# Two blocks of the recurrent branch multiplied between the sparse heads: two transformer blocks in fp32 on one core

## The chip, the core and the metric

One core of a Trainium2 chip runs the whole program. The metric is the device time of one execution in microseconds. Of the kernel before, three runs are shown, with their median.

## What is computed

The reference runs two blocks over 256 tokens of width 1024. The first has a gated and an attention layer, each with a mixture of experts. The second, which matters here, has two layers of feed-forward, hybrid mixer, feed-forward. The mixer projects the normalised tokens once and feeds three branches:

```python
proj = h @ w_in
ret_p, dsa_p, rwkv_p, gate_p = split_cols(proj, GROUP_SIZES)
y_ret  = retention(...)
y_dsa  = sparse_attention(...)      # 8 heads of 64, each query keeps its 64 best keys
y_rwkv = rwkv7_time_mix(rwkv_p, mu, ...)   # recurrent branch
merged = g_ret * (y_ret @ p_ret) + g_dsa * (y_dsa @ p_dsa) + g_rwkv * (y_rwkv @ p_rwkv)
return merged @ w_out
```

`rwkv_p` is 1792 columns of the projection, and the recurrent branch first mixes each of its columns with that of the token before (`p + mu * (prev - p)`). This projection does not depend on the sparse attention.

## The kernel before

The five engines run hand-written streams in fixed order: `pe_...` is TensorE, `v_...` VectorE, `s_...` ScalarE, `g_...` GpSimd and `sp_...` the sync engine's queue. Nothing is scheduled at run time; an engine waits on a semaphore and everything behind it in its stream waits too.

**Weights.** A block is 1024 x 256 weights (1 MB), loaded by the sync queue into a ring of five slots, in a fixed order of jobs; the load of job n goes out when job n-5 has been multiplied, which GpSimd tells the queue (`freed`, L532). The products are made in fp32 out of three reduced products: ScalarE copies the block into a rounded "high part" (`s_part_high`, L2049, the copy at L2058; three buffers, so the high part of load n waits for the product of load n-3), VectorE subtracts it from the weights and leaves the "low part" in the slot (`v_part_low`, L2060, at L2066). `s_ahead(m)` and `v_ahead(m)` (L2078, L2083) do that for load m: "a split" is VectorE's part. TensorE waits for it in `pe_parts`.

**Pieces.** Four PSUM banks are used in turn. Each product that TensorE makes takes the next bank (`take`), after a wait until the piece that had it four pieces ago was read out (`s_free`). Every engine counts all the pieces, and `skip(n)` passes over those that another engine reads. Two more banks hold the sums of the sparse values.

**A block of the branch.** `pe_chan` (L2123) multiplies one block: 2 x 8 x 3 matmuls of 128x128 by 256 columns into one bank. VectorE reads it in `v_shifted_channels` (L3163; two instructions at L3171, two at L3176) with the mixing of neighbours. There are seven such blocks, loads 24 to 30. The first is multiplied between the first two score pairs of the sparse heads, the other six in `pe_rwkv`, after the heads.

**The sparse heads** (`pe_sparse`, L2670; `s_sparse`, `v_sparse`). For heads 0 to 7 in pairs p = 0 to 3:

- `score(p)` makes two pieces, the scores of two heads (`pe_score_pair`, L1168, matmuls of 64x128 by 256);
- VectorE's `softmax_head(h)` adds the mask (L2775, then the bank is free), takes the maximum (L2778) and negates it (L2780);
- ScalarE's `exponential(h)` (L2714) makes the probabilities;
- "the turning" of a head (`pe_turned`, L1182, the transposes at L427) makes one piece, which ScalarE copies out (L2726);
- `values(p)` multiplies the turned probabilities of a pair with the values, in the two banks of the sums.

TensorE's order is score 0, block, score 1, then for each p: turning of heads 2p and 2p+1, values p-1, score p+2; then values 3 and `pe_to_heads`, which spreads the reciprocals of the sums over the channels in two pieces ("the spreading"; it waits for VectorE's reciprocal, L2795). VectorE goes: softmax 0 and 1, read of the first block, softmax 2 to 7, split of load 26, reciprocal. ScalarE's high part 26 (job 26) is made before the exponentials, that of load 27 after the last copy.

Behind the heads the six blocks follow each other in `pe_rwkv` (L2868, the loop at L2887), and in `v_rwkv` (L3180) VectorE takes in turn the split of the load that is wanted two blocks on and the read of a block.

Of the kernel before, what the change touches and what calls it, by code (L numbers as in the profile page):

```python
# [52 lines left out]
DH = 8  # L53
# [23 lines left out]
RW_CHUNKS = 14  # L77
# [122 lines left out]
def build(nc, a, out, regions=("A", "moe0", "B", "moe1", "two"), layers_two=LAYERS):  # L200
    (c1_at, _), (c2_at, _) = constants()
    NC = max(max(v[1] for v in c1_at.values()), max(v[1] for v in c2_at.values()))
    with ExitStack() as ctx:
# [431 lines left out]
        def heads2(b):  # L635

            return ps[:, b, :].rearrange("p (t n) -> p t n", n=BLK)
# [1341 lines left out]
        XLM = lay(KC, SEQ, of=W_parts)  # L1979
# [98 lines left out]
        def s_ahead(*loads):  # L2078
            for m in loads:
                s_part_high()  # L2080
                s.other_jobs(whole_after.get(m, 0))

        def v_ahead(*loads):  # L2083
            for m in loads:
                v_part_low()
                v.other_jobs(whole_after.get(m, 0))
# [583 lines left out]
        def pe_sparse():  # L2670

            pe.e.wait_ge(s_v2p, pe.c["v2p"].next())
            pe.to_channels(DT, KC)
            for n in range(4):

                pe.e.wait_ge(s_free[(pe.pieces.n - 1 - n) % BANKS], pe.read_out(pe.pieces.n - 1 - n))
            pe_scores(range(IH), lambda h: DCT[rows_of(h), 5 + h // 2, :], lambda h: DCT[rows_of(h), 7, :])

            pe_merge_retention()

            def score(p):
                pe_score_pair(p, lambda h: DCT[rows_of(h), h // 2, :], dkey)

            def values(p, turned):
                return pe_value_pair(p, turned,
                                     lambda h: ps[rows_of(h), 4 + h // 4, (h // 2 % 2) * SEQ:(h // 2 % 2 + 1) * SEQ],
                                     lambda h, jt: DTV[:, jt, :], DPTR)

            score(0)
            pe_chan((XH, XLM))  # L2690
            score(1)
            pe.e.wait_ge(s_acc_free, pe.c["accf"].next())
            for p in range(DH // 2):
                turned = [pe_turned(DPRB[:, h]) for h in (2 * p, 2 * p + 1)]
                if p:
                    values(p - 1, held)
                held = turned
                if 2 * p + 4 < DH:
                    score(p + 2)
            values(DH // 2 - 1, held).then_inc(s_acc_full, 1)  # L2700
            pe_to_heads(RCP_TOK)

        def s_sparse():
            copy_channels(s, 0, DCT, KC)
            s.skip(IH)
            s_merge_retention()
            s_ahead(26)
            s.skip(5)

            def exponential(h):  # L2710

                s.e.wait_ge(s_v2a, s.c["v2a"].next())
                for t in range(T):
                    last = nc.scalar.activation(DPRB[:, h, t, :], DSB[:, h % 2, t, :], ACT.Exp, bias=NMX[:, h, t:t + 1],  # L2714
                                                accum_out=LSUM[:, h, t:t + 1])
                last.then_inc(s_exp, 1)

            exponential(0)
            exponential(1)
            for p in range(DH // 2):  # L2720
                for h in (2 * p, 2 * p + 1):
                    if h + 2 < DH:
                        exponential(h + 2)
                    b = s.take()
                    s.e.wait_ge(s_full[b], s.filled())
                    nc.scalar.activation(DPTR[:, h % 4], heads2(b), ACT.Copy).then_inc(s_free[b], 1)  # L2726
                if 2 * p + 4 < DH:
                    s.skip(2)
            s.skip(2)

        def v_sparse():
            BUF["scores"], BUF["ptr"] = DSB, DPTR
            copy_channels(v, 1, DCT, KC)
            for h in range(IH):
                b = v.take()
                v.e.wait_ge(s_full[b], v.filled())
                nc.vector.tensor_scalar(RL[:, :, :], heads2(b), HD ** -0.5, 0.0, ALU.mult, ALU.max).then_inc(s_free[b], 1)
                v.sync()
                for t in range(T):
                    if h == 0:  # L2740
                        nc.vector.tensor_scalar(IS[:, t, :], RL[:, t, :], WI[:, t, h:h + 1], None, ALU.mult)
                    else:
                        nc.vector.scalar_tensor_tensor(IS[:, t, :], RL[:, t, :], WI[:, t, h:h + 1], IS[:, t, :],
                                                       ALU.mult, ALU.add)
                v.sync()
            causal = tab(c2_at, "causal", SEQ)
            nc.vector.tensor_tensor(IS[:, :, :], IS[:, :, :], causal, ALU.add)
            v.sync()

            src = IS  # L2750
            for i in range(TOPK // 8):
                for t in range(T):
                    nc.vector.max(TOP8[:, t, :], src[:, t, :])
                v.sync()
                for t in range(T):
                    nc.vector.match_replace(WORKD[:, t, :], TOP8[:, t, :], src[:, t, :], PAD_LOW)
                v.sync()
                src = WORKD
                v_ahead(18 + i)
                if i % 2:  # L2760
                    v_merge_retention(i // 2)
            nc.vector.tensor_tensor(MASK[:, :, :], WORKD[:, :, :], IS[:, :, :], ALU.not_equal)
            v.sync()
            nc.vector.tensor_scalar(MASK[:, :, :], MASK[:, :, :], -NEG, NEG, ALU.mult, ALU.add)
            v.sync()
            nc.vector.tensor_tensor(MASK[:, :, :], MASK[:, :, :], causal, ALU.add)
            v.sync()
            def softmax_head(h):

                b = v.take()  # L2770
                v.e.wait_ge(s_full[b], v.filled())
                if h >= 2:

                    v.e.wait_ge(s_exp, v.c["exp"].next())
                nc.vector.scalar_tensor_tensor(DSB[:, h % 2], heads2(b), SCALE, MASK[:, :, :],  # L2775
                                               ALU.mult, ALU.add).then_inc(s_free[b], 1)
                v.sync()
                nc.vector.tensor_reduce(MX[:, h, :], DSB[:, h % 2], AX.X, ALU.max)  # L2778
                v.sync()
                nc.vector.tensor_scalar(NMX[:, h, :], MX[:, h, :], -1.0, None, ALU.mult).then_inc(s_v2a, 1)  # L2780

            softmax_head(0)
            softmax_head(1)
            v_shifted_channels(0)
            softmax_head(2)
            softmax_head(3)
            for p in range(2, DH // 2):
                v.skip(2)
                softmax_head(2 * p)
                softmax_head(2 * p + 1)  # L2790
            v_ahead(26)
            v.skip(4)

            v.e.wait_ge(s_exp, v.c["exp"].next(2))
            nc.vector.reciprocal(RCP_TOK.rearrange("p t h -> p h t"), LSUM[:, 0:DH, :]).then_inc(s_v2p, 1)  # L2795
            v.e.wait_ge(s_acc_full, v.c["acc"].next())
            for i in range(2):
                b = v.take()
                v.e.wait_ge(s_full[b], v.filled())
                nc.vector.tensor_copy(flat(RATES[:, :, :]), ps[:, b, :]).then_inc(s_free[b], 1)  # L2800
                v.sync()
                last = nc.vector.tensor_tensor(flat(YTS[:, 2 * i:2 * i + 2, :]), ps[:, 4 + i, :], flat(RATES[:, :, :]),
                                               ALU.mult)
                v.sync()
            nc.vector.nop().then_inc(s_acc_free, 1)

        def g_sparse():
            g.skip(4 + IH)
            g_merge_retention()
            g.skip(2)  # L2810
            g.freed()
            g.skip(2 * DH - 2 + 2)
            g.c["acc"].n += 1


# [52 lines left out]
        def pe_rwkv():  # L2868
# [15 lines left out]
                        last.then_inc(s_gates, 1)  # L2884
                gates_done[0] += count

            for _ in range(RW_CHUNKS // 2 - 1):  # L2887
                pe_chan((XH, XLM))
            pe.e.wait_ge(s_acc_free, pe.c["accf"].peek())
            pe_merge_sparse(0)  # L2890
# [181 lines left out]
            pe.e.wait_ge(s_v2p, pe.c["v2p"].next())  # L3072

        def s_rwkv():
            s.skip(6)
            s_ahead(*range(27, 34))

            s.e.wait_ge(s_v2a, s.c["v2a"].next())
            nc.scalar.activation(LR[0:64, 0, :], LR[0:64, 0, :], ACT.Tanh)
# [98 lines left out]
            last.then_inc(s_free[b], 1)  # L3178

        def v_rwkv():  # L3180
            for c in range(2, RW_CHUNKS, 2):
                v_ahead(26 + c // 2)
                v_shifted_channels(c)
            v.sync()
# [183 lines left out]
            v_part_low()  # L3368

        def g_rwkv():  # L3370
            for _ in range(6):
                g.freed()
            g_merge_sparse(0)
            g.skip(1 + 6 + 4 + 2)
            g_merge_sparse(1)
            g.skip(2)
            g_merge_sparse(2)
            g_merge_sparse(3)
            n_levels = int(math.log2(CH))
            g.skip(6 + WH + 2 + 6 * (n_levels - 2) + 4 + 4 + 6 * N_CH - 4 + 5)  # L3380
# [220 lines left out]
```

## Time and profile before

| | |
|---|---|
| median of 3 runs | 2798.08 us (2797.85 to 2803.94) |
| profiled execution | 2798.51 us, its span 2796.7 us |
| TensorE busy (matmuls) | 2599.5 us, 93% |
| VectorE busy | 1274.0 us, 46% |
| ScalarE busy | 836.0 us, 30% |
| sparse heads and what follows, first layer | from 1576 us on |
| the same, second layer | from 2362 us on |

The profile is of one execution. Times in a timeline are microseconds from the span's start. A group of matmuls starts when its first starts; its last ends some 0.2 us after the next group could start, as matmuls are pipelined, so lengths are best taken from start to start. In square brackets stands how long the engine was idle before, and which engine's instruction ended that. The granted clock (PEclk) is in parts of full speed. A row of the view by stretches has the stretch, its length, the busy time (and number of instructions) of TensorE's matmuls, its weight loads, VectorE, ScalarE and GpSimd, then the clock, the share of the DMA engines' time and the GB/s. A row of DMA issues has the tile and its source, how many, the KB of each and the median time from issue to landing.

### The profile page before, as it was taken

To read this page: it belongs to the slowest core of one execution; us is meant where nothing else is said; L and a number is where in the kernel's file an instruction comes from. 1 tells how busy PE (TensorE), PEld (TensorE's weight loads), DVE (VectorE), ACT (ScalarE), POOL (GpSimd) and SP (SyncE) were. 2 spreads that over 40 slices of the span, in tenths; PEclk is the share of its full clock that TensorE was granted. 3 is DMA by queue.
4 is the path that set the end of the run, shared out by engine and by line. 5 is a ranking of instruction groups with operands and counts; after the bars stand their busy time and mean duration, and the time that the engine had idled before them with its cause. 6 is when DMAs were issued, how large, how long until landed. Compare 5 with 4: busy or idle time off the path is not lost.

```text
span 2796.7 us, 46123 instructions
## 1 busy us (share of the span) xinstructions
PE 2599.5 (93%) x19503; PEld 2008.1 (72%) x19503; DVE 1274.0 (46%) x1875; ACT 836.0 (30%) x1051; POOL 0.2 (0%) x4
## 2 busy tenths in 40 slices
PE   8899888879899888879999999999999999999998
PEld 8743433348543333369999899999899898899998
DVE  4610101037411000055566765655655658766555
ACT  4300000025210000033343442443433444523433
POOL 0000000000000000000000000000000000000000
PEclk9999999999999999999999999999999999999999
DMA  8689999973899999955563441455555544323553
GB/s 270 264 357 425 426 425 425 426 286 106 329 400 425 425 425 425 426 192 181 181 230 122 135 140 59 137 166 181 181 181 181 192 152 150 107 77 107 166 181 136
DMA packets 286519, 685.17 MB, mean 245 GB/s; under 512 B 11992, under 2 KB 217616, under 8 KB 236944
## 3 DMA queue, kind: packets, MB, share of 16 engines
q1 hardware_dynamic: 282792, 671.27, 63.6%
q10 hardware_dynamic: 3560, 11.45, 1.1%
q8 instruction: 132, 2.16, 0.3%
q14 instruction: 35, 0.29, 0.0%
HBM read 681.63 MB, written 1.05 MB: 244 GB/s over the span
## 4 chain that ended last, share of the span: by engine, by line
PE 69%; DMA 20%; DVE 6%; ACT 2%; issue 1%; DVEq 1%; SPq 0%; ACTq 0%; POOLq 0%
PE psum L419 68%; DMA weight_ring<-in_w_gate 14%; DMA weight_ring<-in_w_up 3%; DMA weight_ring<-in_w_down 2%; DVE weight_ring_parts L2066 1%; PE psum L427 1%; ACT weight_ring_parts L2058 1%; DVEq L552 1%; DMA weight_ring<-in_w_in_a 0%; DVE arena L3260 0%; SPq L1921 0%; DMA h_tok<-in_mem 0%; DMA weight_ring<-in_w_in 0%; DVE arena L1837 0%; DVE small L2778 0%
## 5 line engine op out<-in xcount | busy, mean ns | idle before, releaser
L419 PE MATMUL psum<-weight_ring_parts,arena_parts 128*128 128x256 f32 (+1 forms) x2992 | 666.4, 315 | 6.3 <-DVE arena_parts L2159 1.9
L2066 DVE TENSOR_TENSOR weight_ring_parts<-weight_ring,weight_ring_parts 128x2048 fp32r<-128x2048 f32 x217 | 496.5, 2290 | 338.0 <-ACT weight_ring_parts L2058 332.0
L419 PE MATMUL psum<-x_chan_parts,weight_ring_parts 128*128 128x256 f32 x3200 | 612.2, 282 | 12.9 <-DVE arena_parts L2155 7.7
L2058 ACT ACTIVATE weight_ring_parts<-weight_ring 128x2048 fp32r<-128x2048 f32 x217 | 414.9, 1913 | 465.7 <-POOLq L532 345.4
L419 PE MATMUL psum<-weight_ring,arena 128*64 128x512 f32 (+1 forms) x2112 | 474.8, 582 | 73.8 <-DMA weight_ring<-in_w_gate 39.1
L419 PEld LDWEIGHTS psum<-weight_ring_parts,arena_parts 128*128 128x128 f32 x2992 | 496.4, 189 | 42.9 <-issue 3.3
L419 PEld LDWEIGHTS psum<-x_chan_parts,weight_ring_parts 128*128 128x128 f32 x3200 | 509.0, 190 | 18.3 <-issue 12.9
L419 PE MATMUL psum<-arena 64*64 64x64 f32 (+7 forms) x4616 | 467.0, 335 | 29.3 <-DVE arena L1837 15.6
L419 PEld LDWEIGHTS psum<-weight_ring,arena 128*64 128x64 f32 (+1 forms) x2112 | 179.3, 140 | 361.4 <-issue 358.5
L419 PE MATMUL psum<-weight_ring_parts,x_chan_parts 128*128 128x256 f32 x2336 | 427.5, 285 | 2.3 <-DVE arena_parts L2155 2.2
L419 PE MATMUL psum<-arena_parts,weight_ring_parts 128*128 128x256 f32 x1536 | 419.0, 283 | 0.0
L419 PEld LDWEIGHTS psum<-arena 64*64 64x64 f32 (+3 forms) x4616 | 247.6, 141 | 227.9 <-issue 210.1
L419 PEld LDWEIGHTS psum<-weight_ring_parts,x_chan_parts 128*128 128x128 f32 x2336 | 359.3, 189 | 10.0 <-issue 7.8
L419 PEld LDWEIGHTS psum<-arena_parts,weight_ring_parts 128*128 128x128 f32 x1536 | 284.1, 189 | 1.3
L1853 DVE TENSOR_TENSOR arena<-arena,psum 128x512 f32<-128x512 f32 x32 | 22.0, 687 | 521.2 <-PE psum L419 519.9
L1837 DVE COPY arena<-psum 128x512 f32<-128x512 f32 x48 | 33.2, 691 | 296.9 <-PE psum L419 262.5
L1699 ACT ACTIVATE arena<-psum 128x512 f32<-128x512 f32 x32 | 19.1, 597 | 484.6 <-PE psum L419 484.6
L1692 ACT ACTIVATE arena<-psum 128x512 f32<-128x512 f32 (+1 forms) x80 | 34.3, 467 | 371.8 <-PE psum L419 335.0
L2066 DVE TENSOR_TENSOR weight_ring_parts<-weight_ring,h_tok_parts 128x2048 fp32r<-128x2048 f32 x32 | 73.3, 2291 | 66.6 <-ACT h_tok_parts L2058 65.8
L419 PE MATMUL psum<-arena_parts,h_tok_parts 128*128 128x256 f32 x320 | 90.2, 282 | 0.0
L419 PE MATMUL psum<-x_chan_parts,h_tok_parts 128*128 128x256 f32 x320 | 89.7, 280 | 0.0
L427 PE MATMUL psum<-tables,arena 128*128 128x128 f32 x472 | 69.9, 288 | 14.9 <-DVE arena_parts L2159 4.6
(324 smaller groups left out, 1713.6 us busy)
## 6 DMA issues: line engine op xcount, KB each, us to landing
weight_ring<-in_w_gate SPq DMA_DIRECT2D x92, 1024.0 KB, 23.2
weight_ring<-in_w_up SPq DMA_DIRECT2D x92, 1024.0 KB, 22.9
weight_ring<-in_w_in SPq DMA_DIRECT2D x70, 1024.0 KB, 5.0
arena<-in_w_down SPq DMA_DIRECT2D x64, 1024.0 KB, 22.5
weight_ring<-in_w_down SPq DMA_DIRECT2D x64, 1024.0 KB, 23.2
weight_ring<-in_ffa_w_in SPq DMA_DIRECT2D x44, 1024.0 KB, 7.1
weight_ring<-in_ffb_w_in SPq DMA_DIRECT2D x44, 1024.0 KB, 5.7
arena<-in_w_gate SPq DMA_DIRECT2D x36, 1024.0 KB, 18.5
```

Of the source, the lines that this page charges most:

```text
L419: return nc.tensor.matmul(*args, **kw)
L427: last = nc.tensor.transpose(ps[0:cols, b, lo:lo + rows], src, ident[0:rows, 0:rows])
L552: self.e.drain()
L1692: nc.scalar.activation(dst, ps[:, b, 0:dst.shape[1]], ACT.Copy).then_inc(s_free[b], 1)
L1699: nc.scalar.activation(SILU[:, half, :], ps[:, b, :], ACT.Silu).then_inc(s_free[b], 1)
L1837: nc.vector.tensor_copy(dst, ps[:, b, :]).then_inc(s_free[b], 1)
L1853: nc.vector.tensor_tensor(HG[:, half * 512:(half + 1) * 512], SILU[:, half, :], ps[:, b, :], ALU.mult).then_inc(s_free[b], 1)
L2058: nc.scalar.activation(HIGH[buf], ring[:, sl, :], ACT.Copy).then_inc(s_hi, 1)
L2066: nc.vector.tensor_tensor(ring_parts[:, sl, :], ring[:, sl, :], f32(HIGH[buf]), ALU.subtract).then_inc(s_split, 1)
```

## The change

Two of the six `pe_chan` calls move from `pe_rwkv` into the loop over the pairs: one at p = 0 and one at p = 2, each behind the turnings and the values of the round, ahead of `score(p + 2)` where there is one. On ScalarE the high parts of loads 27 and 28 move to behind the first two exponentials and behind the copies of p = 1. On VectorE the split of load 26 moves to behind the read of the first block; the read of the second block and the split of load 27 stand around softmax 4 and 5, the split of load 28 and the read of the third block behind softmax 7. The `skip` and `freed` calls of each stream follow the new order of pieces. Nothing is computed otherwise.

```diff
--- before.py
+++ after.py
@@ -2695,6 +2695,8 @@
                 if p:
                     values(p - 1, held)
                 held = turned
+                if p in (0, 2):
+                    pe_chan((XH, XLM))
                 if 2 * p + 4 < DH:
                     score(p + 2)
             values(DH // 2 - 1, held).then_inc(s_acc_full, 1)
@@ -2717,6 +2719,7 @@
 
             exponential(0)
             exponential(1)
+            s_ahead(27)
             for p in range(DH // 2):
                 for h in (2 * p, 2 * p + 1):
                     if h + 2 < DH:
@@ -2724,6 +2727,10 @@
                     b = s.take()
                     s.e.wait_ge(s_full[b], s.filled())
                     nc.scalar.activation(DPTR[:, h % 4], heads2(b), ACT.Copy).then_inc(s_free[b], 1)
+                if p == 1:
+                    s_ahead(28)
+                if p in (0, 2):
+                    s.skip()
                 if 2 * p + 4 < DH:
                     s.skip(2)
             s.skip(2)
@@ -2782,14 +2789,21 @@
             softmax_head(0)
             softmax_head(1)
             v_shifted_channels(0)
+            v_ahead(26)
             softmax_head(2)
             softmax_head(3)
-            for p in range(2, DH // 2):
-                v.skip(2)
-                softmax_head(2 * p)
-                softmax_head(2 * p + 1)
-            v_ahead(26)
-            v.skip(4)
+            v.skip(2)
+            v_shifted_channels(2)
+            softmax_head(4)
+            softmax_head(5)
+            v_ahead(27)
+            v.skip(2)
+            softmax_head(6)
+            softmax_head(7)
+            v_ahead(28)
+            v.skip(2)
+            v_shifted_channels(4)
+            v.skip(2)
 
             v.e.wait_ge(s_exp, v.c["exp"].next(2))
             nc.vector.reciprocal(RCP_TOK.rearrange("p t h -> p h t"), LSUM[:, 0:DH, :]).then_inc(s_v2p, 1)
@@ -2809,7 +2823,11 @@
             g_merge_retention()
             g.skip(2)
             g.freed()
-            g.skip(2 * DH - 2 + 2)
+            g.skip(2 + 2)
+            g.freed()
+            g.skip(4 * 2)
+            g.freed()
+            g.skip(2 + 2)
             g.c["acc"].n += 1
 
 
@@ -2884,7 +2902,7 @@
                         last.then_inc(s_gates, 1)
                 gates_done[0] += count
 
-            for _ in range(RW_CHUNKS // 2 - 1):
+            for _ in range(RW_CHUNKS // 2 - 3):
                 pe_chan((XH, XLM))
             pe.e.wait_ge(s_acc_free, pe.c["accf"].peek())
             pe_merge_sparse(0)
@@ -3072,8 +3090,8 @@
             pe.e.wait_ge(s_v2p, pe.c["v2p"].next())
 
         def s_rwkv():
-            s.skip(6)
-            s_ahead(*range(27, 34))
+            s.skip(4)
+            s_ahead(*range(29, 34))
 
             s.e.wait_ge(s_v2a, s.c["v2a"].next())
             nc.scalar.activation(LR[0:64, 0, :], LR[0:64, 0, :], ACT.Tanh)
@@ -3178,7 +3196,7 @@
             last.then_inc(s_free[b], 1)
 
         def v_rwkv():
-            for c in range(2, RW_CHUNKS, 2):
+            for c in range(6, RW_CHUNKS, 2):
                 v_ahead(26 + c // 2)
                 v_shifted_channels(c)
             v.sync()
@@ -3368,7 +3386,7 @@
             v_part_low()
 
         def g_rwkv():
-            for _ in range(6):
+            for _ in range(4):
                 g.freed()
             g_merge_sparse(0)
             g.skip(1 + 6 + 4 + 2)
```

## Rows read from the trace of the kernel before

**Rows 1.** The page, part 1: busy time, share, instructions of TensorE.

```profile
PE 2599.5 (93%) x19503; PEld 2008.1 (72%) x19503; DVE 1274.0 (46%) x1875; ACT 836.0 (30%) x1051; POOL 0.2 (0%) x4
```

**Rows 2.** The view by stretches, the eight heads in each layer.

```profile
1583.40:1602.00 18.60, 14.00 (x122) 9.43 (x121) 13.80 (x25) 12.85 (x37) 0.00 (x0) 1.00 0.17 57
2369.17:2387.70 18.53, 13.94 (x121) 9.39 (x120) 13.77 (x25) 12.50 (x35) 0.00 (x0) 1.00 0.18 57
```

**Rows 3.** The timeline of TensorE, first layer: start, duration, engine, line, [idle before].

```profile
1583.40 1.13 PE L419 MATMUL psum<-arena 64*128 64x256 f32 x8
1584.46 0.66 PE L427 MATMUL psum<-tables,arena 128*128 128x128 f32 x4
1585.49 0.63 PE L427 MATMUL psum<-tables,arena 128*128 128x128 f32 x4 [0.36 <-DVE arena L3176]
1587.74 1.13 PE L419 MATMUL psum<-arena 64*128 64x256 f32 x8 [1.63 <-DVE arena L2775]
...
1590.37 0.63 PE L427 MATMUL psum<-tables,arena 128*128 128x128 f32 x4 [0.91 <-ACT arena L2726]
1590.93 2.15 PE L419 MATMUL psum<-arena 128*64 128x256 f32 x16
1593.01 0.66 PE L427 MATMUL psum<-tables,arena 128*128 128x128 f32 x4
...
1597.66 0.66 PE L427 MATMUL psum<-tables,arena 128*128 128x128 f32 x4 [1.00 <-ACT arena L2714]
1598.24 2.04 PE L419 MATMUL psum<-arena 128*64 128x256 f32 x16
1600.08 1.95 PE L419 MATMUL psum<-tables,small 128*64 128x128 f32 x32
1601.96 0.39 PE L419 MATMUL psum<-x_chan_parts,weight_ring_parts 128*128 128x256 f32 x1
```

**Rows 4.** The timeline of VectorE behind the heads.

```profile
1607.92 0.88 DVE L3171 TENSOR_SCALAR arena<-psum,small 128x256 f32<-128x256 f32 x2 [1.22 <-PE psum L419]
...
1613.57 0.87 DVE L3171 TENSOR_SCALAR arena<-psum,small 128x256 f32<-128x256 f32 x2 [1.30 <-PE psum L419]
```

**Rows 5.** The timeline of VectorE in the heads.

```profile
1583.51 0.88 DVE L3171 TENSOR_SCALAR arena<-psum,small 128x256 f32<-128x256 f32 x2 [0.60 <-PE psum L419]
...
1585.26 0.68 DVE L2775 SCALAR_TENSOR_TENSOR arena<-psum,arena 128x512 f32<-128x512 f32 x1
...
1586.90 0.69 DVE L2775 SCALAR_TENSOR_TENSOR arena<-psum,arena 128x512 f32<-128x512 f32 x1
...
1588.45 0.17 DVE L2780 TENSOR_SCALAR small<-small 128x2 f32<-128x2 f32 x1
...
1596.38 2.28 DVE L2066 TENSOR_TENSOR weight_ring_parts<-weight_ring,weight_ring_parts 128x2048 fp32r<-128x2048 f32 x1
1598.59 0.25 DVE L2795 RECIPROCAL small<-small 128x16 f32<-128x16 f32 x1
```

**Rows 6.** The timeline of ScalarE in the heads.

```profile
1588.65 0.51 ACT L2714 ACTIVATE arena<-arena,small 128x256 f32<-128x256 f32 x1
...
1589.65 0.57 ACT L2726 ACTIVATE arena<-psum 128x512 f32<-128x512 f32 x1
...
1598.94 1.91 ACT L2058 ACTIVATE weight_ring_parts<-weight_ring 128x2048 fp32r<-128x2048 f32 x1
```

**Rows 7.** The timeline of the sync queue before the heads.

```profile
1576.63 0.37 SPq L500 DMA_DIRECT2D weight_ring<-in_w_in  x1
```

**Rows 8.** The DMA view, 1565 to 1612 us: the loads of that time.

```profile
weight_ring<-in_w_in SPq DMA_DIRECT2D x5, 1024.0 KB, 4.9
```

**Rows 9.** The timeline of TensorE at the stage's entry.

```profile
1524.39 2.90 PE L427 MATMUL psum<-tables,arena 128*128 128x128 f32 x14 [2.29 <-DVE arena_parts L2159]
```

**Rows 10.** The view by stretches, TensorE's clock behind that wait.

```profile
1525.00:1528.00 3.00, 2.72 (x13) 2.32 (x12) 2.03 (x5) 1.75 (x5) 0.00 (x0) 0.50 0.00 2
1524.00:1529.00 5.00, 3.76 (x20) 3.26 (x22) 3.55 (x8) 2.75 (x5) 0.00 (x0) 0.66 0.15 51
```


## The prediction

> **What bounds the kernel now.** I went from the page to the stretches. On the page TensorE is busy 93% of the span [rows 1]: the kernel is bound by TensorE nearly everywhere, so an edit that leaves TensorE's work as it was can gain only where TensorE waits. The change touches one such stretch, once per layer: the eight sparse heads. The view by stretches shows it [rows 2]: from the second score pair to the first block of the recurrent branch TensorE is busy 14.00 of 18.60 us in the first layer and 13.94 of 18.53 in the second. So 4.6 us per layer, 9.2 in both, is all that there is to fill (0.4 of it, before the turning of head 1, stays in any case). TensorE's timeline [rows 3] shows where it lies: 1.63 us before the third score pair (its banks wait for VectorE's reads of the second pair), 0.91 before the turning of head 3, 1.00 before that of head 7, the rest in small pieces. The clock is 1.00 in these stretches, the 2.4 GHz level.
>
> Of the work behind it: once the heads are done TensorE multiplies six blocks of the recurrent branch without a gap; VectorE's reads of two of them start 1613.57 - 1607.92 = 5.65 us apart [rows 4], which is a block's length. At that pace VectorE has per block one split (2.29) and one read (1.83), 4.1 of 5.65 us: it is not the bound there, so taking two blocks from it gives nothing by itself.
>
> **Unit times** (starts to starts, first layer). TensorE [rows 3]: score pair 1584.46 - 1583.40 = 1.06; turning of one head 1590.93 - 1590.37 = 0.56; value pair plus score pair 1593.01 - 1590.93 = 2.08, so a value pair 1.02; the last two value pairs together 1600.08 - 1598.24 = 1.84; spreading the reciprocals 1601.96 - 1600.08 = 1.88. VectorE [rows 5]: the read of a block 1585.26 - 1583.51 = 1.75 until the next operation starts (1.83 until its bank is free: the turning of head 1 starts at 1585.49 [rows 3], less 0.15); a split 1598.59 - 1596.38 = 2.21; a head's softmax step 1586.90 - 1585.26 = 1.64, its bank free 0.69 after its start, its negated maximum issued 1588.45 - 1586.90 = 1.55 after it. ScalarE [rows 6]: the exponential starts 1588.65 - 1588.45 = 0.20 after that, takes 1.00, the copy behind it 0.57; a high part 1.91. From a bank freed by VectorE to TensorE's start: 1587.74 - (1586.90 + 0.69) = 0.15 [rows 3, 5].
>
> **The change, part by part.** TensorE's instructions are the same in number and kind: two blocks of 5.65 leave the row behind the heads and stand inside. I follow the first layer from 1583.40 on; nothing before it moves, except that VectorE has a split to do behind its first read.
>
> *First block (behind the turnings of heads 0 and 1).* These end at 1585.49 + 0.56 = 1586.05. The block's weights were split long before: the split that is moved is the one two blocks on. But the block takes the bank of head 2's scores, and VectorE reads these only after its first block and the new split: split from 1585.26, softmax of head 2 from 1585.26 + 2.21 = 1587.47, bank free 1588.16, TensorE goes at 1588.31. So the gap of 1.69 (by starts) is not filled but becomes 2.26; the split is what is new on the path. The block ends at 1593.96, and the score pair is done at 1595.02.
>
> *Turnings 2 and 3.* The first ends at 1595.58. The second takes the bank of the block, which VectorE reads from 1594.07 to 1595.90: it goes at 1596.05, a new wait of 0.47, in place of the 0.9 that stood there for ScalarE. The value pair ends at 1597.63.
>
> *Score pair 4.* Its banks are those of heads 4 and 5, whose softmax VectorE now starts only behind the read: 1595.82 and 1597.46, free 1598.15, TensorE 1598.30, a new wait of 0.67. During the block VectorE had stood idle some 3 us, since all it could read was read. Done at 1599.36.
>
> *Turnings 4 and 5.* The second needs the copy of turned head 3, which stands in ScalarE's queue behind the exponential of head 5: negated maximum 1597.46 + 1.55 = 1599.01, exponential 1599.21 to 1600.21, copy until 1600.78, TensorE 1600.93. The turning of head 4 was done at 1599.92: a wait of 1.0. Value pair done at 1602.51.
>
> *Second block.* VectorE splits from 1599.08, softmax 6 from 1601.29, bank free 1601.98: before 1602.51, no wait, by 0.4 us. Block until 1608.16. Under it ScalarE and VectorE finish heads 6 and 7 and the third split (until about 1606.8), so both turnings, the two value pairs and the spreading run without a wait: 1608.16 + 2 x 0.56 + 1.84 + 1.88 = 1613.00. VectorE reads the block from 1608.27 to 1610.10 and the reciprocal behind it is out before the spreading begins at 1611.12.
>
> *ScalarE and the queues.* Its high part for load 27 falls in its pause until the exponential of head 2 and costs nothing; that for load 28 (1.91) stands before the exponential of head 6, until about 1602.7, and that head's maximum is out at 1601.29 + 1.55 = 1602.84: nothing, and under the second block anyway. The loads are issued from the sync queue when a block five jobs back is done: load 28 at 1576.63 [rows 7], on the chip 4.9 us later [rows 8], 19 us before it is wanted; load 29 follows at the end of the first block of the branch, unchanged. GpSimd only passes on that a slot is free; its waits follow the same order of pieces. Later loads are issued up to 14 us earlier; nothing else uses the queue there.
>
> *Behind the heads.* Four blocks follow instead of six. VectorE has the splits of the first two of them done (loads 27, 28), and load 29's is ready 5 us before its block. So the row runs at 5.65 as before.
>
> **The sum.** Old: the third block starts at 1601.96 + 2 x 5.65 = 1613.26. New: 1613.00. The gain is 0.3 us, against 4.6 that was there: by starts, waits of 1.69, 1.00, 0.42, 0.43 and 1.10, together 4.6, go, and 2.26, 0.47, 0.67 and 1.0, together 4.4, come. The second layer has the same stretch [rows 2] and gives the same: 0.5 us in both. Against the profiled execution's 2798.51 (its span of 2796.70 and 1.81 around it) that is 2798.0; the median of the runs shown, 2798.08, lies 0.4 lower, so I forecast 2797.6. About 0.3% (8.4 us) is what a measurement of this kernel can tell from no change.
>
> **A rule against the change.** Up to 1524.39 TensorE waited 2.29 us before a turning, and then [rows 9] ran at 0.50, the 1.2 GHz level, for 3 us and more [rows 10]; 1.63 us of waiting in the heads did not do that. My new longest gap, 2.26, is close to the one that did. The Trainium skill's page TensorE: Matmul & The Clock Gate (section "A second HAM failure mode: psum-queue depth-cycling") says that short idles between groups of matmuls, as banks are cycled, can make the clock swing between its levels. By that rule the block behind the gap would be partly slow; the heads before, with six waits, show the opposite so far.
>
> **Rivals.**
> A: *the waits are really filled.* If VectorE's split costs TensorE nothing (another bank order than I read, or blocks long enough that everything is ready), the 4.6 us per layer go: 2797.6 + 0.5 - 9.2 = 2788.9, just over 0.3% faster. For it: the second block does just that. Against it: the first block's bank is freed by a read behind the new split. A middle case, half of it, is 2793.5.
> B: *VectorE's single queue makes it slower.* Place: the read of the first block, between softmax 3 and 4. While TensorE multiplies, VectorE idles, and afterwards read (1.83) and two softmax steps (2 x 1.64 less what is hidden) must pass before score pair 4, and the copy of head 3 before turning 5. I have 0.47 + 0.67 + 1.0 of waits there; if the whole chain of 1.83 + 3.28 shows less the value pair and the turnings that run beside it (1.02 + 0.56), it is 3.5, 1.4 more per layer, and if the margin of 0.4 before the second block is lost to a full split as well (2.2 - 0.4), 3.2 more. It is slower than before once the new waits pass 4.6 per layer, which is 0.3 us above my sum. Time: 2797.6 + 2 x 1.4 = 2800.4, with the second 2804.0, still within 0.3%.
> C: *the clock falls behind the new gap.* In rows 10 the mean clock over 5 us is 0.66, which loses 5 x 0.34 = 1.7 us; once per layer: 2797.6 + 3.4 = 2801.0.
> D: *the edit moves nothing*, since the product waits for its weights. Excluded in time: load 28's copy ends long before, as above. An extreme on this side would be both new splits and reads fully exposed, 2 x (2.29 + 1.83) = 8.2 per layer, 16.5 in all: 2814.
>
> **How the numbers follow.** Forecast (within 2 us of 2797.6): 0.62. A in full 0.03, its middle case 0.08. B 0.17, mostly under 2804. C 0.07. D and the unforeseen 0.03. The range takes the middle case of A and B with its second part: 2793.5 to 2804.0; no more than 1 in 10 is outside. Faster by over 0.3%: 0.03. Slower by over 0.3%: 0.03. Within: 0.94.
>
> **What would show it.** In TensorE's timeline of the new kernel: a gap of 2.2 us before the first inner block, put down to VectorE's softmax; 0.3 to 0.5 before turning 3 put down to the read of the block; 0.6 to 0.7 before score pair 4; 0.9 before turning 5 put down to ScalarE's copy; none from the second block to the third. From the second score pair to the first block behind the heads 29.6 us, in place of 18.56. The clock stays 1.00. Wrong would be: a stretch under 27 us (A) or over 31 (B), a clock of 0.50 in it (C), or a gap behind the heads.

## The result, and the profile of the changed kernel

| | before | changed |
|---|---|---|
| median | 2799.54 us (20 runs, 2797.77 to 2810.67) | 2805.87 us (20 runs, 2802.49 to 2809.12) |
| ratio | | 1.0017, 95% interval 1.0010 to 1.0024 |
| profiled execution | 2798.51 us, span 2796.7 | 2808.27 us, span 2806.5 |
| granted clock, mean over the span | 0.987 | 0.981 |

The change makes the kernel slower by 0.17%, 4.8 us by the ratio (2.8 to 6.7 by its interval), 6.3 us by the medians. That is within the 0.3% that I had called no change, but the median lies 1.9 us above the range that I gave.

The page of the changed kernel: the head and TensorE's row, which answers to [rows 1]. The instructions are as many as before, and TensorE is busy 13.6 us longer with them.

```profile
span 2806.5 us, 46123 instructions
...
PE 2613.1 (93%) x19503; PEld 2020.3 (72%) x19503; DVE 1273.9 (45%) x1875; ACT 835.7 (30%) x1051; POOL 0.2 (0%) x4
```

TensorE's timeline of the changed kernel, first layer, without the matmuls inside a block (answers to [rows 3]; in brackets the idle time before and what ended it). `L2782` is the softmax's first operation, L2775 before.

```profile
1589.32 1.14 PE L419 MATMUL psum<-arena 64*128 64x256 f32 x8
1590.38 0.66 PE L427 MATMUL psum<-tables,arena 128*128 128x128 f32 x4
1591.41 0.63 PE L427 MATMUL psum<-tables,arena 128*128 128x128 f32 x4 [0.37 <-DVE arena L3194]
1594.21 0.35 PE L419 MATMUL psum<-x_chan_parts,weight_ring_parts 128*128 128x256 f32 x1 [2.17 <-DVE arena L2782]
...
1601.57 1.13 PE L419 MATMUL psum<-arena 64*128 64x256 f32 x8
1602.63 0.66 PE L427 MATMUL psum<-tables,arena 128*128 128x128 f32 x4
1603.65 0.63 PE L427 MATMUL psum<-tables,arena 128*128 128x128 f32 x4 [0.37 <-DVE arena L3194]
...
1605.91 1.13 PE L419 MATMUL psum<-arena 64*128 64x256 f32 x8 [0.61 <-DVE arena L2782]
1606.97 0.66 PE L427 MATMUL psum<-tables,arena 128*128 128x128 f32 x4
1608.54 0.63 PE L427 MATMUL psum<-tables,arena 128*128 128x128 f32 x4 [0.91 <-ACT arena L2729]
...
1610.11 0.39 PE L419 MATMUL psum<-x_chan_parts,weight_ring_parts 128*128 128x256 f32 x1
...
1615.87 1.03 PE L427 MATMUL psum<-tables,arena 128*128 128x128 f32 x8
1616.83 1.98 PE L419 MATMUL psum<-arena 128*64 128x256 f32 x16
1618.62 1.95 PE L419 MATMUL psum<-tables,small 128*64 128x128 f32 x32
1620.49 0.39 PE L419 MATMUL psum<-x_chan_parts,weight_ring_parts 128*128 128x256 f32 x1
```

Every wait of the prediction's order is there, at its place and put down to the engine that was named: 2.17 us before the first inner block, 0.37 before the turning of head 3, 0.61 before score pair 4, 0.91 before the turning of head 5, and none from the second block to the third. What is not as forecast is the length of the first block: 1601.57 - 1594.21 = 7.36 us in place of 5.65. The second takes 1615.87 - 1610.11 = 5.76. The view by stretches of the changed kernel says why (columns as in [rows 2]; the last but two is the granted clock):

```profile
1592.00:1594.00 2.00, 0.03 (x1) 0.00 (x0) 2.00 (x2) 0.00 (x0) 0.00 (x0) 1.00 1.02 358
1594.60:1598.00 3.40, 3.40 (x18) 3.40 (x17) 1.90 (x5) 2.80 (x10) 0.00 (x0) 0.50 0.00 0
1609.60:1616.00 6.40, 6.40 (x56) 6.02 (x53) 4.53 (x6) 3.75 (x11) 0.00 (x0) 1.00 0.01 3
```

While TensorE waits the clock is still 1.00; behind the wait it is 0.50, the 1.2 GHz level, for 3.4 us, with TensorE busy all the time. So 1.7 us are lost, and from the second score pair to the third block in order it is 1620.49 - 1589.32 = 31.17 us, against 29.60 forecast and 18.56 + 2 x 5.65 = 29.86 before. In the second layer the wait is there again, 2.17 us, and the clock falls again.

VectorE's timeline of the changed kernel (answers to [rows 5]):

```profile
1591.17 2.28 DVE L2066 TENSOR_TENSOR weight_ring_parts<-weight_ring,weight_ring_parts 128x2048 fp32r<-128x2048 f32 x1
1593.37 0.69 DVE L2782 SCALAR_TENSOR_TENSOR arena<-psum,arena 128x512 f32<-128x512 f32 x1
...
1601.67 0.88 DVE L3189 TENSOR_SCALAR arena<-psum,small 128x256 f32<-128x256 f32 x2 [4.93 <-PE psum L419]
...
1603.42 0.68 DVE L2782 SCALAR_TENSOR_TENSOR arena<-psum,arena 128x512 f32<-128x512 f32 x1
...
1606.69 2.29 DVE L2066 TENSOR_TENSOR weight_ring_parts<-weight_ring,weight_ring_parts 128x2048 fp32r<-128x2048 f32 x1
1608.89 0.69 DVE L2782 SCALAR_TENSOR_TENSOR arena<-psum,arena 128x512 f32<-128x512 f32 x1
```

The split (2.28 us) stands between the read of the block and the softmax of head 2; only when that has read its scores is the bank free (1593.37 + 0.69) and TensorE goes 0.15 us later. Then VectorE idles 4.93 us under the block: the split would have fitted there.

The two profiled executions differ by 9.8 us in their spans, and most of that is not the change's. The second score pair of the first layer starts at 1589.32 against 1583.40 before, and up to there both kernels run the same instructions: 5.9 us. The two heads' stretches give 1.3 us each, and 1.3 us lie between them and behind them.

### The profile page after: what moved, and what is told of

The parts are those of the page before. It is cut to its first block, busy times and chain, and to the rows that moved or that the text cites. A ratio compares the mean times of both kernels' runs of the same rounds, so it can differ in the third digit from the quotient of the medians.

```text
span 2806.5 us, 46123 instructions
## 1 busy us (share of the span) xinstructions
PE 2613.1 (93%) x19503; PEld 2020.3 (72%) x19503; DVE 1273.9 (45%) x1875; ACT 835.7 (30%) x1051; POOL 0.2 (0%) x4
## 4 chain that ended last, share of the span: by engine, by line
PE 70%; DMA 20%; DVE 6%; ACT 2%; issue 1%; DVEq 1%; SPq 0%; ACTq 0%; POOLq 0%
PE psum L419 68%; DMA weight_ring<-in_w_gate 14%; DMA weight_ring<-in_w_up 3%; DMA weight_ring<-in_w_down 2%; DVE weight_ring_parts L2066 1%; PE psum L427 1%; ACT weight_ring_parts L2058 1%; DVEq L552 1%; DMA weight_ring<-in_w_in 0%; DVE arena L3278 0%; DMA h_tok<-in_mem 0%; SPq L1921 0%; PE psum L686 0%; DVE arena L1837 0%; DVE arena_parts L2155 0%
## 5 line engine op out<-in xcount | busy, mean ns | idle before, releaser
L419 PE MATMUL psum<-arena 64*64 64x64 f32 (+7 forms) x4616 | 468.9, 336 | 27.4 <-DVE arena L1837 15.7
L2058 ACT ACTIVATE h_tok_parts<-weight_ring 128x2048 fp32r<-128x2048 f32 x32 | 61.1, 1911 | 72.5 <-POOLq L532 36.3
```

Of the source, the lines that this page charges most:

```text
L419: return nc.tensor.matmul(*args, **kw)
L2058: nc.scalar.activation(HIGH[buf], ring[:, sl, :], ACT.Copy).then_inc(s_hi, 1)
```

## The experiments

To compare kernels with one, two or three blocks inside, I take the time from the second score pair to the third block behind it in order, whichever place that has: "the stretch". Where fewer or more blocks lie inside, 5.65 us per block are added or taken off. All figures of the stretch are of the first layer of the profiled execution, unless the second is named; 29.86 us before, 31.17 changed. A ratio is that against the kernel before in the same measurement; microseconds "by the ratio" are worked out from it.

### The changed kernel twice more

The kernel is not edited; it is measured again, twice.

> The changed kernel once more, to see whether its clock falls again in the same place. Theory 1 (the clock): the new wait of 2.2 us before the first inner block brings TensorE to 0.50 for 3.4 us in each layer, 1.7 us lost per layer against 0.3 won by the order: about 3 us slower than before from the heads, and both falls are in the profile again. Theory 2 (chance): the falls of the first profile were an accident; the profile has none or one of them, and the kernel is within 1 us of before. Theory 3 (something outside the heads): slower by 5 us or more again, and the difference of the two profiles lies outside the heads.

Measured: 2804.97 us (11 runs) against 2803.16 before (27 runs), ratio 1.0012 (1.0003 to 1.0021), 3.4 us by the ratio and 1.8 by the medians.

> The changed kernel for a third profile. Theory 1: a fall of 3.4 us in the heads of each layer again; 1.3 us lost per layer there; 2.6 us slower than before plus what its falls elsewhere differ by. If the difference to the kernel before is again 3.4 to 4.8 us, something outside the heads takes 1 to 2 us on average; the profile shows where.

Measured: 2805.24 us (11 runs) against 2799.91 (31 runs), ratio 1.0017 (1.0008 to 1.0026). In both profiles the wait of 2.17 us is there and the block behind it runs partly at 0.50, in both layers. In the three profiles of the changed kernel that is six falls out of six. Theory 2 (chance) is out for the falls in the heads. In the experiments 27 to 33 runs of before stand beside each kernel, and their median moves between 2799.9 and 2803.2, so the ratios say more than the medians; where the two differ by much, both are given.

### The kernel before once more

> The kernel before once more, as a kernel of its own, for a second profile of it: where its clock falls outside the heads, and whether ever inside them. Theory 1: none inside the heads (its longest wait there is 1.63 us); falls elsewhere come and go from run to run, some us in all. Time as the kernel before, within 0.5 us.

Measured: 2800.21 us (11 runs) against 2799.91, ratio 0.9998 (0.9989 to 1.0007). In its profile, as in the first one of before, the clock stays 1.00 through the heads of both layers. Outside them it falls in several places, [rows 9, 10] one of them, and not the same ones each time; the spans of the two profiles of the same kernel differ by 1.8 us. A wait at the entry of the second layer's mixer went both ways: it is 2.50 us long in the first profile of before and 2.51 in the second, and the clock fell behind it in the second alone (0.59 from 2199.60 to 2203.00). From the first profile, the row of waits, with their sum, number and longest, and two stretches:

```profile
PE psum L686 <- DVE h_tok L2028: 2.9, 2, 2.5
2195.00:2200.00 5.00, 2.14 (x14) 1.43 (x14) 3.12 (x6) 2.89 (x6) 0.00 (x0) 1.00 1.08 351
2200.00:2205.00 5.00, 3.61 (x31) 3.40 (x30) 3.22 (x8) 4.83 (x9) 0.00 (x0) 1.00 0.13 41
```

### The wait filled with useless matmuls

```diff
+                if p == 0:
+                    for i in range(18):
+                        pe.mm(ps[:, 6, 0:SEQ], XH[:, i % KC, 0:P], XH[:, i % KC, :], start=True, stop=True)
                 if p in (0, 2):
                     pe_chan((XH, XLM))
```

> Changed kernel; in the wait of 2.2 us before the first inner block TensorE multiplies 18 matmuls of the blocks' own kind (128x128 by 256 columns) into a PSUM bank that nothing reads then, 2.1 us of work. Theory 1 (the clock falls because TensorE idles there): the block starts when it did, the falls behind the heads' wait are gone, and 1.7 us per layer come back: 3.4 us faster than the changed kernel, about as fast as before. Theory 2 (the clock falls for another reason, or does not cost): same time as the changed kernel, or slower by up to 0.3 us per layer where the matmuls overrun the wait.

Measured: 2799.50 us (11 runs) against 2800.09 before (33 runs), ratio 0.9998 (0.9988 to 1.0009). TensorE's timeline of this kernel, from the turning of head 1 on:

```profile
1585.96 1.13 PE L419 MATMUL psum<-arena 64*128 64x256 f32 x8
...
1588.04 0.63 PE L427 MATMUL psum<-tables,arena 128*128 128x128 f32 x4 [0.36 <-DVE arena L3197]
1588.43 2.40 PE L419 MATMUL psum<-x_chan_parts 128*128 128x256 f32 x18
1590.84 0.36 PE L419 MATMUL psum<-x_chan_parts,weight_ring_parts 128*128 128x256 f32 x1
...
1596.68 1.14 PE L419 MATMUL psum<-arena 64*128 64x256 f32 x8
...
1613.73 1.95 PE L419 MATMUL psum<-tables,small 128*64 128x128 f32 x32
1615.60 0.39 PE L419 MATMUL psum<-x_chan_parts,weight_ring_parts 128*128 128x256 f32 x1
```

and its view by stretches around the block, in both layers:

```profile
1588.00:1597.00 9.00, 8.94 (x73) 8.64 (x75) 5.25 (x8) 3.55 (x11) 0.00 (x0) 1.00 0.30 106
2373.00:2382.00 9.00, 8.97 (x76) 8.47 (x74) 5.27 (x9) 3.15 (x10) 0.00 (x0) 1.00 0.24 83
```

The 18 matmuls run in the wait, the block starts at 1590.84 and takes 1596.68 - 1590.84 = 5.84 us at a clock of 1.00, and the stretch is 1615.60 - 1585.96 = 29.64 us: the forecast of 29.60. More work, put where TensorE idled, makes the kernel faster by 0.14% to 0.19% (the ratio of 0.9998 against the changed kernel's 1.0012 and 1.0017, which were measured at other times). So it is the idle time, and through the clock, that makes the changed kernel's heads slower than before; its order alone is worth as good as nothing. By these ratios the gain over the changed kernel is 3.9 to 5.3 us, more than the 2 x 1.53 = 3.1 that the stretches give; the rest is not explained.

### The split behind softmax 3

```diff
             v_shifted_channels(0)
-            v_ahead(26)
             softmax_head(2)
             softmax_head(3)
+            v_ahead(26)
```

> Changed kernel, only the split of load 26 on VectorE behind the softmax of heads 2 and 3 instead of ahead of it. The bank of the first inner block is then free at once. Theory 1: the wait of 2.2 us and with it the fall of the clock go: second score pair to the first block behind the heads 29.6 - 2.2 = 27.4 us, clock 1.00; about 5 us faster than before, some 8 to 10 faster than the changed kernel. Theory 2 (no clock effect, the order alone): 4.4 us faster than the changed kernel, no more. Theory 3: it stays slower than before.

Measured three times, with 11 runs each: 2797.12 us against 2803.16, ratio 0.9987 (0.9978 to 0.9996);

> The changed kernel with the split of load 26 behind softmax 3, once more, beside the next one. Again 4 to 6 us faster than before, no fall of the clock inside the heads.

2797.84 against 2800.09, ratio 0.9988 (0.9979 to 0.9998);

> Two blocks inside with the split of load 26 behind softmax 3, beside the other three: 2.4 us shorter per layer than before, 4.9 us faster; between 4 and 6 by the median.

2798.90 against 2799.91, ratio 0.9989 (0.9980 to 0.9999). By the ratios that is 3.1 to 3.6 us faster than before where 4.9 were forecast, which each interval takes in (0.3 to 6.2 us over the three). By the medians it is 6.0, 2.3 and 1.0 us, so the last two fall short of the 4 to 6 expected. TensorE's timeline of the first of them:

```profile
1584.56 1.13 PE L419 MATMUL psum<-arena 64*128 64x256 f32 x8
...
1586.65 0.63 PE L427 MATMUL psum<-tables,arena 128*128 128x128 f32 x4 [0.36 <-DVE arena L3194]
...
1593.07 1.13 PE L419 MATMUL psum<-arena 64*128 64x256 f32 x8
...
1595.16 0.63 PE L427 MATMUL psum<-tables,arena 128*128 128x128 f32 x4 [0.37 <-DVE arena L3194]
...
1597.42 1.13 PE L419 MATMUL psum<-arena 64*128 64x256 f32 x8 [0.61 <-DVE arena L2782]
...
1600.04 0.63 PE L427 MATMUL psum<-tables,arena 128*128 128x128 f32 x4 [0.90 <-ACT arena L2729]
...
1610.12 1.94 PE L419 MATMUL psum<-tables,small 128*64 128x128 f32 x32
1612.00 0.38 PE L419 MATMUL psum<-x_chan_parts,weight_ring_parts 128*128 128x256 f32 x1
```

The first block follows the turning of head 1 at once, and the stretch is 1612.00 - 1584.56 = 27.44 us against 27.4 forecast, in each of the three profiles and both layers (2.42 less than before). VectorE now splits under the block:

```profile
1586.42 0.68 DVE L2782 SCALAR_TENSOR_TENSOR arena<-psum,arena 128x512 f32<-128x512 f32 x1
...
1588.07 0.69 DVE L2782 SCALAR_TENSOR_TENSOR arena<-psum,arena 128x512 f32<-128x512 f32 x1
...
1589.69 2.29 DVE L2066 TENSOR_TENSOR weight_ring_parts<-weight_ring,weight_ring_parts 128x2048 fp32r<-128x2048 f32 x1
```

### One block alone, the first or the second

```diff
-                if p in (0, 2):
+                if p == 0:
                     pe_chan((XH, XLM))
```

The other kernel has `if p == 2` there. In it VectorE's splits 26 and 27 both stand behind softmax 7.

> Only the first of the two blocks is moved (pair 0), with the split of load 26 where the change has it; the second stays behind the heads. The wait of 2.2 us is there, and the turnings of heads 6 and 7 wait as before. By the steps of the prediction the third block starts 2.4 us later per layer than before: 4.9 us slower from the order. Theory 1: another 1.7 per layer from the clock, 8 us slower. Theory 2: 5 us slower.

Measured: 2811.11 us (5 runs) against 2803.16, ratio 1.0042 (1.0028 to 1.0055), or 11.8 us; by the medians 8.0, with 8 expected. The stretch is 34.04 us, 4.2 longer than before: the 2.4 of the order and 1.7 of the clock. In the second layer the first wait did not bring the clock down, but the turnings of heads 6 and 7 did, behind waits of 1.60 and 0.99 us with four small matmuls between; behind the same two waits of the first layer it stayed 1.00. TensorE's timeline there, and the clock:

```profile
2395.77 0.66 PE L427 MATMUL psum<-tables,arena 128*128 128x128 f32 x4 [1.60 <-ACT arena L2716]
2397.42 0.66 PE L427 MATMUL psum<-tables,arena 128*128 128x128 f32 x4 [0.99 <-ACT arena L2716]
2398.01 3.23 PE L419 MATMUL psum<-arena 128*64 128x256 f32 x16
```

```profile
2398.60:2402.00 3.40, 3.40 (x24) 2.27 (x22) 0.00 (x0) 2.02 (x2) 0.00 (x0) 0.51 0.02 5
```

> Only a block at pair 2 is moved (the second block of the branch); all of VectorE's splits stand behind softmax 7, none ahead of softmax 2. The waits before the turnings of heads 6 and 7 (0.4 and 1.1 us) are filled, the others stay as before, the longest 1.63. Theory 1: the clock stays 1.00, 1.5 us per layer are won: 3 us faster than before. Theory 2: the same. Theory 3 (a block inside costs what it fills): no faster than before.

Measured: 2799.11 us (11 runs) against 2803.16, ratio 0.9992 (0.9983 to 1.0001). The stretch is 28.20 us, 1.66 shorter than before, and the clock stays 1.00: the second block does fill the waits of 0.37 and 1.00 us. Over two layers that is 3.3 us; the ratio gives 2.2, and its interval includes no gain.

### The split alone, no block moved

```diff
             v_shifted_channels(0)
+            v_ahead(26)
             softmax_head(2)
...
-            v_ahead(26)
             v.skip(4)
```

> Kernel before; no block is moved, only VectorE's split of load 26 stands behind the read of the first block instead of behind softmax 7. Order of VectorE alone: the third score pair waits 2.2 us longer (3.9 in place of 1.7), all else of the heads follows, and behind them nothing comes back, since that split was hidden: 4.4 us slower than before in both layers. Theory 1 adds the clock behind the longer wait: some 3.4 more, 7 to 8 us slower. Theory 2: 4.4 us slower.

Measured: 2809.18 us (10 runs) against 2800.09, ratio 1.0030 (1.0019 to 1.0041), or 8.4 us. TensorE's timeline and clock behind the wait:

```profile
1593.71 2.08 PE L419 MATMUL psum<-arena 64*128 64x256 f32 x8 [3.83 <-DVE arena L2775]
1595.72 1.97 PE L427 MATMUL psum<-tables,arena 128*128 128x128 f32 x8
```

```profile
1593.70:1600.20 6.50, 6.49 (x28) 4.17 (x30) 3.84 (x8) 4.99 (x18) 0.00 (x0) 0.51 0.00 0
```

The wait is 3.83 us, the clock stays at half for 6.5 us and more, and the stretch is 4.1 us longer in the first layer, 5.2 in the second: 2.2 of the order, the rest of the clock, which in the second layer fell once more behind waits of 0.82 and 0.99 us. All of that comes from where one split of 2.3 us stands on VectorE.

### Three blocks inside

```diff
-                if p in (0, 2):
+                if p in (0, 1, 2):
                     pe_chan((XH, XLM))
```

with the splits on VectorE behind softmax 3, 5 and 7 (two there), ScalarE's high part of load 29 behind the copies of p = 2, and the reads of the blocks in the order of their pieces.

> As the one before it, with three blocks inside: at pairs 0, 1 and 2, each behind the values; VectorE splits 26 behind softmax 3, 27 behind softmax 5, 28 and 29 behind softmax 7. The waits before score pair 4 (0.6 us) and the turning of head 5 (0.9) fall mostly under the block at pair 1. By the steps of the prediction the fourth block starts 1.2 us earlier per layer than with two inside: 2.4 us faster than that, about 7 us faster than before, if the clock stays. If the waits only move elsewhere: no difference from two inside.

Measured: 2797.68 us (12 runs) against 2800.09, ratio 0.9986 (0.9977 to 0.9995): no measurable difference from two inside, where 7 us less than before was forecast. The stretch is 27.14 us, 0.3 less than with two in the first layer, and 27.54, 0.1 more, in the second, in place of the 1.2 less forecast. TensorE's timeline shows the new wait:

```profile
1615.67 1.97 PE L419 MATMUL psum<-tables,small 128*64 128x128 f32 x32 [0.55 <-DVE small L2813]
```

The spreading waits for the reciprocal, which stands behind VectorE's split of load 29, and that had itself waited 1.25 us for ScalarE's high part. In the second layer the spreading waits 0.90 us. The last kernel moves that split behind the reciprocal and the head sums:

```diff
-            v_ahead(29)
             v_shifted_channels(6)
...
         def v_rwkv():
+            v_ahead(29)
             for c in range(8, RW_CHUNKS, 2):
```

> Three blocks inside as before, but VectorE's split of load 29 behind the reciprocal and the head sums, instead of ahead of the read of the last inner block. In the last kernel the spreading waited 0.55 us for the reciprocal behind that split. If that is all: the stretch shortens by 0.55 per layer against three inside, 3.3 per layer shorter than before, 6.6 us in both, and 1.7 faster than two inside with the split behind softmax 3. If not: nothing changes.

Measured: 2793.35 us (9 runs) against 2799.91, ratio 0.9975 (0.9965 to 0.9985): 7.0 us faster than before, 6.6 by the medians. Its page:

```profile
span 2789.7 us, 46123 instructions
```

The stretch is 26.41 us, 3.45 less than before in each layer, where 3.3 was forecast, and the wait for the reciprocal is gone. This is the fastest of the kernels, 0.4% faster than the changed one.

## Why the prediction was wrong

**The order of the heads** was right term by term. I had 2.26, 0.47, 0.67 and 1.0 us of new waits by starts; the profile has 2.17, 0.37, 0.61 and 0.91 in its brackets, which leave out some 0.1 us each of matmuls running out, and no wait where I had none. With the wait filled, and the clock thereby kept up, the stretch is 29.64 us against my 29.60. That VectorE's new split, and not the block, decides the first wait is shown by its move behind softmax 3: 2.2 us less, as computed.

**The step that failed** is the one under "A rule against the change": the sum takes the clock to stay at its upper level behind a wait of 2.2 us, and so has no term for it. I had a row for each side, 2.29 us of waiting that brought it down [rows 9, 10] and 1.63 us that did not [rows 3], and my own longest gap came to within 0.1 us of the one that did. By the nearest row the fall was the likely case, and I gave it 0.07. Rival C was the outcome. Its price was right in the stretch (1.7 us per layer forecast, 31.17 - 29.60 = 1.57 in the profile). But the rows also show that such a wait need not bring a fall: the profile of before has four waits of 2.29 to 2.52 us behind stretches at full clock, ended at 1412.13, 1524.39, 2198.19 and 2309.92 us, and the clock fell behind three of them. Nor does 1.63 us mark the safe side: a wait of 1.88 us near 99 us was followed by a fall in the second profile of before, and by none in the first.

The Trainium skill's page TensorE: Matmul & The Clock Gate (section "A second HAM failure mode: psum-queue depth-cycling") ties such swings to frequent short idles between groups of matmuls. The trace agrees that waiting between two groups can bring the clock down, here one wait of 2.17 us in six layers of six; that frequent short waits do it the heads of before do not show, where six waits of 0.33 to 1.63 us left the clock at 1.00 in four layers.

**The total** is not fully explained. The heads lose 1.3 us per layer against before, 2.6 in all. That lies inside the intervals of the two repeats (0.8 to 5.9 us and 2.2 to 7.3) and just under that of the first result (2.8 to 6.7); the three ratios stand at 3.4 to 4.8. Outside the heads the clock falls in different places from one profile to the next, in the kernel before too, at the entries of stages. The spans of the changed kernel's three profiles differ by 5 us (2806.5, 2802.4, 2801.4) with the same heads; ahead of the second score pair of the first layer alone, where nothing was changed, they differ by 4.8 us (1589.32, 1584.87, 1584.55). Between the stretches of the two layers, with the moved blocks allowed for, the three take 1.0, 1.7 and 1.1 us more than before, but kernels without a fall in the heads take from 1.1 us less to 3.5 more. At the entry of the second layer's mixer all three of the changed kernel fell and one of two of the kernel before; kernels without the wait in the heads show both. Whether a shift of 1 or 2 us in the heads makes later falls likelier, or a mean of 1 to 2 us is chance, is open: too few profiles tell it.

**The range** was too low for a second reason: I set it on the three runs shown, of which two were at 2798. Over 20 runs the median of the same kernel is 2799.5, and beside the first experiments 2803.2. The clock alone would have left the result inside the range: heads slower by 2.6 us in place of faster by 0.5 make 2797.6 + 3.1 = 2800.7, which is rival C's 2801.0. The median of before was 1.5 us higher than the one that I had, and the 3.7 us left to 2805.87 (2.2 by the ratio, 4.8 less 2.6) are the open part above. The spread upwards (to 2811) was to be had neither from the profile nor from three runs, but a highest of 2803.94 among three should have moved the upper end.

**Rival A** (the waits really filled) describes in part the kernels with the split elsewhere: 4.8 us of the 9.2 with two blocks, 6.9 with three, in the stretches. **Rival B** did not come: between the read of the first block and the turning of head 5 the waits are those of the sum.

## What to carry to other kernels

Filling a TensorE wait with independent work is worth what the work's own conditions leave: here the block needed a bank that VectorE freed only behind a split put in at the same time, so the wait moved and grew from 1.63 to 2.17 us. On an engine that works in fixed order, put a long preparation (2.3 us) behind the short operations that free a bank for TensorE, under the long product: here that alone was worth 3.7 us per layer in the stretch (31.17 against 27.44). And when a gap in TensorE's work comes near the length of one that brought the clock down elsewhere in the same trace, look up every gap of that length there, and give the fall the chance that they show, here three in four.

## What was not expected of the hardware

- In the heads a wait of 2.17 us brought the clock to half in 6 of 6 layers of the changed kernel and in 1 of 2 with only the first block moved. Waits of 1.60 and 0.99 us with a turning of four small matmuls between them did so in one of two layers; in the kernel before, 0.37 and 1.00 us with a turning between never did in four layers.
- The same wait of 2.50 us in the same kernel was followed by a fall in one profile and by none in another. The wait of 2.29 us of [rows 9] was followed by one in all 14 profiles, and the same wait in the second layer in 13 of 14.
- 18 matmuls whose result nobody reads, 2.4 us of TensorE's time, made the stretch of the changed kernel 1.5 us shorter in each layer.
- A wait of 3.83 us was followed by 6.5 us and more at half clock, one of 2.17 us by some 3.4 us.
